# Two transformer blocks in fp32 on one core: pair sums every ten steps, earlier splits of the down weights, and another order of a norm's parts

## The reference, cut to what matters

```python
mod = jnp.dot(jax.nn.silu(c), w_ada) + b_ada
...
merged = jax.nn.sigmoid(ga) * y_a + jax.nn.sigmoid(gb) * y_r
x = x + gate1 * jnp.dot(merged, w_out)
h2 = _rmsnorm(x, norm2_w) * (1.0 + scale2) + shift2
ffn = jnp.dot(jax.nn.silu(jnp.dot(h2, w_ffn_gate)) * jnp.dot(h2, w_ffn_up), w_ffn_down)
x = x + gate2 * ffn
return _rmsnorm(x, final_norm_w)
```

## Time and profile before

| what | value |
|---|---|
| median of 3 runs | 1520.65 us (1519.39 to 1521.84) |
| profiled execution | 1521.84 us |
| its span | 1520.0 us |
| granted TensorE clock, mean | 0.994 |
| TensorE busy | 1488.0 us (98%) |
| VectorE busy | 1107.5 us (73%) |
| ACT busy | 710.9 us (47%) |

### The profile page before, as it was taken

One profiled execution on the slowest core, in us unless ns is written; L12 is line 12 of the kernel. 1 busy time (PEld: TensorE's weight loads), 2 busy tenths in 40 slices (PEclk: granted clock), 3 DMA queues, 4 the chain that ended last, 5 costly groups with the idle time before them and its releaser, 6 DMA issues.

```text
span 1520.0 us, 22717 instructions
## 1 busy us (share of the span) xinstructions
PE 1488.0 (98%) x9247; PEld 1248.8 (82%) x9247; DVE 1107.5 (73%) x1841; ACT 710.9 (47%) x1158; POOL 64.2 (4%) x93
## 2 busy tenths in 40 slices
PE   7999999999999999999999889999999999999999
PEld 5777888778877899999988777777788988888887
DVE  6669888875587698888789766787567456556885
ACT  4453334653221365455465553766525334434653
POOL 1000000000000011000000112200011000000000
PEclk9999999999999999999999989999999999999999
DMA  9423124358687678967357417850114232233473
GB/s 386 146 76 99 62 69 140 112 177 308 224 292 278 231 262 245 256 173 188 98 165 218 150 32 245 180 111 30 57 56 129 93 109 83 86 111 97 135 230 127
DMA packets 87025, 238.09 MB, mean 157 GB/s; under 512 B 12037, under 2 KB 12165, under 8 KB 85769
## 3 DMA queue, kind: packets, MB, share of 16 engines
q1 hardware_dynamic: 68312, 204.87, 39.5%
q0 software_dynamic: 18608, 31.77, 9.8%
HBM read 222.94 MB, written 45.35 MB: 177 GB/s over the span
## 4 chain that ended last, share of the span: by engine, by line
PE 85%; DVE 9%; ACT 2%; DMA 2%; issue 1%; POOL 0%; SPq 0%; DVEq 0%; ACTq 0%
PE bank L831 81%; PE bank L843 4%; DVE AR L2144 2%; DVE wl L2110 1%; DMA CST<-in_down 1%; DVE ACC L2107 1%; DVE Hl L2144 1%; ACT wh L1544 1%; DVE AR L2454 1%; DVE CST L2144 1%; DVE X L2144 0%; DVE G L2151 0%; DMA raw<-in_wst 0%; DMA X<-in_x 0%; DVE AR L2151 0%
## 5 line engine op out<-in xcount | busy, mean ns | idle before, releaser
L1544 ACT ACTIVATE wh<-raw 128x1024 fp32r<-128x1024 f32 (+1 forms) x248 | 259.0, 1046 | 335.4 <-PE bank L831 284.7
L2110 DVE TENSOR_TENSOR wl<-raw,wh 128x1024 fp32r<-128x1024 f32 (+1 forms) x248 | 297.2, 1208 | 96.9 <-ACT wh L1544 96.8
L831 PE MATMUL bank<-wh,Hh 128*128 128x512 f32 (+1 forms) x732 | 296.1, 405 | 1.5 <-DVE Hl L2144 0.7
L831 PE MATMUL bank<-wh,Hl 128*128 128x512 f32 (+1 forms) x732 | 283.9, 388 | 0.0
L831 PE MATMUL bank<-Hh,wh 128*128 128x256 f32 (+2 forms) x824 | 279.1, 339 | 4.6 <-DVE wl L2110 3.0
L831 PE MATMUL bank<-wl,Hh 128*128 128x512 f32 (+1 forms) x732 | 283.3, 387 | 0.0
L831 PE MATMUL bank<-Hl,wh 128*128 128x256 f32 (+2 forms) x824 | 277.1, 336 | 0.0
L831 PE MATMUL bank<-Hh,wl 128*128 128x256 f32 (+2 forms) x824 | 277.0, 336 | 0.0
L831 PEld LDWEIGHTS bank<-Hh,wh 128*128 128x128 f32 (+1 forms) x824 | 156.5, 190 | 22.4 <-DVE wl L2110 3.4
L831 PEld LDWEIGHTS bank<-Hl,wh 128*128 128x128 f32 (+1 forms) x824 | 156.5, 190 | 16.6 <-issue 0.5
L831 PEld LDWEIGHTS bank<-Hh,wl 128*128 128x128 f32 (+1 forms) x824 | 156.4, 190 | 16.5
(11 more groups left out here) (298 smaller groups left out, 2365.8 us busy)
## 6 DMA issues: line engine op xcount, KB each, us to landing
raw<-in_wst SPq DMA_DIRECT2D x212, 512.0 KB, 4.5
sums_dram<-in_down POOLq DMA_DIRECT2D x11, 2816.0 KB, 32.8
raw<-sums_dram SPq DMA_DIRECT2D x37, 512.0 KB, 4.1
raw<-in_down SPq DMA_DIRECT2D x25, 512.0 KB, 4.4
CST<-in_down SPq DMA_DIRECT2D x11, 1024.0 KB, 6.0
sums_dram<-CST SPq DMA_DIRECT2D x11, 1024.0 KB, 4.6
AR<-in_wst SPq DMA_DIRECT2D x8, 1024.0 KB, 10.5
CST<-in_wst SPq DMA_DIRECT2D x10, 512.0 KB, 6.5
```

Of the source, the lines that this page charges most:

```text
L831: return e.matmul(o, l, r, start=start, stop=stop, skip_group_check=True)
L1544: e.activation(HI[slot[i]][:, 0:width(i)], raw_of(i), ACT.Copy).then_inc(*w_hi.mark(i))
L2110: e.tensor_tensor(LO[slot[i]][:, 0:n], raw_of(i), HI[slot[i]][:, 0:n].bitcast(f32), SUB).then_inc(*w_lo.mark(i))
```

## The change

It has five edits.

1. The chunks of `ada` parts 4 and 5 enter the weight plan one chunk of gb1 earlier (`start=1`).
2. `summing()` places a pair's load, additions and store every ten steps instead of twelve, the additions still six steps behind the load.
3. In `schedule()` the down product takes two splits in a step from s = 4 on. The later splits and the loads of SP for them stand two steps earlier than before.
4. On VectorE, `after_dn(0)` and `after_dn(1)` are both called behind the two `upper_rows`, so that both tiles' additions stand ahead of both norms. On ACT, the square of tile 2 is placed one step after the call instead of three.
5. SP issues the loads of two bias rows (`row(4)`, `row(5)`) earlier in gb0.

```diff
@@ -84,7 +84,7 @@
     w_in("gr0 gr1 ga0 ga1", ada((2, 3), 1))
     w_in("gb0")
     among = ada((4, 5), 1)
-    block("gb1", "w_in", 8, [(6728, 512)], among=among, start=2)
+    block("gb1", "w_in", 8, [(6728, 512)], among=among, start=1)
     for n in (0, 1):
         block(f"ap{n}", "w_attn_proj", 4, [(512 * n, 512)], among=among)
     for n in (0, 1):
@@ -206,9 +206,9 @@
     load, add, store = ([[] for _ in range(len(ticks) + 2)] for _ in range(3))
     among = [k for k, t in enumerate(ticks) if t[0] in EARLY]
     for p in range(11):
-        load[among[12 * p]].append(("dn", p))
-        add[among[12 * p + 6]].append(("dn", p))
-        store[among[12 * p + 6]].append(("dn", p))
+        load[among[10 * p]].append(("dn", p))
+        add[among[10 * p + 6]].append(("dn", p))
+        store[among[10 * p + 6]].append(("dn", p))
     return load, add, store
 
 
@@ -418,7 +418,7 @@
                 ahead = 5 if name != "iq" else 3 if what[0] == 7 else what[0] % 2
                 if not avail or rank[at] > here + ahead + 3 * (name == "up"):
                     break
-                if name == "dn" and hi_at[k]:
+                if name == "dn" and len(hi_at[k]) > (what[0] > 3):
                     break
                 soon = at in (i, ticks[k + 1][2])
                 if mine and loaded.get(at, -9) + 2 > k and not soon:
@@ -1893,7 +1893,7 @@
                     on.wait_ge(*dve.of(("dn", "left", 20)))
                     e.activation(xn, X[:, t, :], ACT.Square, scale=1.0 / 32, accum_out=ss).then_inc(*act.mark(("last", "mean", t)))
                 if t == 2:
-                    w.after(3, root)
+                    w.after(1, root)
                 else:
                     root()
                 w.after((3, 4, 4, 4)[t], lambda: norm_root("n3", t, dve.of(("last", "x", t))))
@@ -2758,7 +2758,9 @@
                         added(SGR[2 + r], SGR[2 + r], "5", r, "v")
                     if s == 35:
                         w.after(3, lambda r=r: upper_rows(r))
-                        after_dn(r)
+                        if r:
+                            after_dn(0)
+                            after_dn(1)
                     if s == (42, 47)[r]:
                         added(SGR[r], SGR[r], "4", r, "c21 4")
                         gated(SGR[r], 0, 2 + r, ("dn", "x", 2 + r))
@@ -3262,9 +3264,9 @@
                         compression(2)
                         on.wait_ge(*small.of(("comp", 0)))
                         compression(3)
-                    if name == "gb0" and what == (2, 0):
+                    if name == "gb0" and what == (1, 3):
                         row(4)
-                    if name == "gb0" and what == (2, 2):
+                    if name == "gb0" and what == (2, 1):
                         row(5)
                     if name == "2dn" and what[0] in FINISHED:
                         event, rows, h, n = FINISHED[what[0]]
```

## The result

| | before | changed |
|---|---|---|
| median | 1519.97 us (1518.82 to 1521.84, 6 runs) | 1526.45 us (1523.54 to 1531.46, 6 runs) |
| ratio of the times | | 1.0043, 95% interval 1.0024 to 1.0062 |
| profiled execution, its span | 1521.84, 1520.0 us | 1523.63, 1521.8 us |

The changed kernel is 6.5 us slower by the medians, where 2.6 us of gain were forecast. Its times are spread over 8 us, those of before over 3. The profiled execution of the changed kernel is one of its two fastest and that of the kernel before is its slowest, so the two profiles show only a part of the loss, 1.8 us, but they show where it lies.

A forecast was written before the change was run, and what follows sets the result against it. TensorE, busy 98% of the span, was taken as the bound, so only its waits and low clock could be regained. Region 2's -2.1 and region 1's -0.5 gave -2.6 us from the median 1520.65: 1518.1 us, range 1513.6 to 1522.8.

The forecast's parts named there:

- Region 2: Down product's end and its norms: norm_scale(2) and TensorE's turn 2 come sooner, -2.1 us (bounds -1.0 and -3.5).
- the wait before turn 0: Third norm: TensorE waits some 4.1 us for norm_scale(0), where it lost 5.2 before; slow matmuls stay.
- POOL and the lock: Rival at the norms: POOL done only with the additions, norms 1.2 us later, 1519.3 us in all; chance 0.10.
- Region 1: Stretch with pairs every ten steps: four terms for sums ahead of what TensorE needs, -0.5 us (bounds -6.4 and +6).
- (a): Sum at 443.76, ahead of a bank read: it stands earlier; of TensorE's 1.6 us wait 0.8 is gained.
- (d): Pair 10's sum at step 290, just before wo0's wl: new wait, 0.7 us lost.
- Part 3: Pairs every ten steps: SP stands about 1.5 us at nearly every pair load, raw weight loads queued behind.
- (b): wl at 475.10, ending the 3.0 us wait: one sum comes ahead, another goes; -1.1 us (ends -4.8 and +0.6).
- (c): Pair 4's sum ahead of a wl of gb1, near 400: new wait, 0.7 us lost.
- The signs of being wrong: TensorE waits less than 2 us before turn 0, or the sums' load waits grow with each pair.
- The rival that came true: Slower by the buffer's round: above 14.8 us, each pair later, sums meet wl of gb1, rp1, wo0; +5.7, written 1525; chance 0.12.
- The page's price for 1 MB: Pair loads: 4.4 us each by the page, a round of 11.5 us, region 1 would give 4 us; not used.

The follow-up runs named there:

- e1: Kernel before with only the three edits of the down product (two splits a step, additions ahead of norms, third square sooner): 1517.72 us, ratio 0.9988.
- e5: Kernel before with only two splits a step in the down product; norms stay between the additions, third square late: 1521.70 us, ratio 1.0012.
- e3: Kernel before with only the pairs placed every ten steps instead of twelve: 1528.50 us, ratio 1.0055.
- e16: Kernel before with pair 1's load one step sooner, exchanged with ga1.2's raw load on SP's queue, nothing else: 1525.30 us, ratio 1.0032.
- e15: Kernel before with pairs every ten steps, loads after the first two steps later (10p + 2), sums and stores at 10p + 8: 1528.54 us, ratio 1.0048.
- e10: Kernel before with pairs every ten steps, but pair 1 left at its old place (12 and 18): 1526.72 us, ratio 1.0041.
- e13: Kernel before with pair 1's load at step 10 instead of 12, its sum at 16, and half that load's bytes: 1524.75 us, ratio 1.0021.
- e4: Kernel before with only the ada chunks one place sooner and the bias rows sooner, pairs every twelve steps: 1520.89 us, ratio 0.9995.
- e7: Kernel before with only the third tile's square two steps sooner: 1519.88 us, ratio 0.9994.
- e17: e10 with pair 6's load four steps later, behind five raw loads, its sum three later, pairs 7 and 8 shifted: 1533.51 us, ratio 1.0080.
- e11: Kernel before with every pair's sum and store eight steps behind the load instead of six, spacing twelve: 1518.31 us, ratio 0.9980.
- e2: Kernel before with only the three stream edits (pairs every ten steps, ada chunks and bias rows sooner): 1529.84 us, ratio 1.0060.

## Why the prediction was wrong

**Region 2, -2.1 us:** right in mechanism, somewhat small. Additions, `last_norm`, both norm scales and the wait before turn 0 came within 1 us of their forecast places. Turn 2 came 2.4 us sooner for 2.1. The rest of the 3.2 measured is the clock: the wait before turn 2 was 2.6 us instead of 3.9, and the slow matmuls behind it cost 0.8 less, where I had kept them all. I had the wait as longer than before because TensorE would be 3 us ahead; it was 1.0 ahead. The low clock now covers the transposes of turns 0 and 1: their rows take 1.97 and 1.84 us, before 1.04 and 1.03. e1 gives 3.0 in the median and 1.8 by the ratio. e5 confirms that splitting sooner does not by itself gain the 5.2 us.

**POOL and the lock:** no sign of starvation. The rival that POOL ends only with the last addition is refuted: `last_norm(0)` started straight behind the last addition, with no idle time for POOL. In the changed kernel POOL's second operation takes 0.99 us beside the additions and 0.57 alone, so it is held for some 0.4 us and not to the end of the row.

**Region 1, -0.5 us:** this step failed; it measured +5.8 in the trace and +7.8 in e3's median. The sum of terms (a) to (d) looked only at what stands behind a sum on VectorE. It left out the queue on which the moved load is issued. Part 3 said that SP would stand "with the loads of raw weights queued behind it", and put no price on it. The largest loss, 4.5 us in the trace and 4.9 by e16, comes of it: pair 1's load passes ga1.2's. The next, 1.9 us at 431, is on the same queue: a raw load behind a pair load for which SP stood. The trace of before had the evidence: ACT already waited 1.69 us for ga1.2's data at 347.40, so this load had no slack, and the order of SP shows what overtakes it. Of the terms: (a) the gap at 445 fell from 1.6 to 1.0 us, and the stretch around it gained 0.3, where I took 0.8; (b) the wait at rp1.3 is 2.7 for 3.0 us, worth 0.4, and its slow matmuls stay, where I took 1.1, and executions of one program differ there by more; (c) near 400 and (d) at wo0 there is no stall in the changed kernel's trace, both were 0 of the 0.7 each; (d)'s stall did appear in e15.

The signs of being wrong did not show it either: TensorE waited 3.4 us before turn 0, and the sums' waits did not grow from pair to pair (4.3, 0, 3.2, 0, 1.7, 7.9, 0, 0.7, 3.0, 0 and 1.4 us). SP stood for the store at 7 pair loads and not at 11. No sign watched the raw loads.

**The rival that came true** had its chance at 0.12, its price about right (+5.7; 6.5 measured) and its mechanism half right: VectorE stood at sums (22.1 us for 13.8) and raw loads queued behind. It had each pair later than the one before, by rounds above the spacing, and the sums head on against `wl` of gb1, rp1 and wo0; the trace has one such round in eleven and no new stall at these three. It missed the overtaken load, so that its price came out is in part luck. The range ended at 1522.8, half way to this rival's 1525, though region 1's own bound of +6 with region 2's -2.1 gives 1524.6; the measured 1526.45 is beyond that too.

**The page's price for 1 MB** (4.4 us by the Trainium skill's fit, "DMA: Bandwidth & Descriptors", "Anatomy of one DMA — SWDGE (gpsimd) path", for the other kind of queue) was rightly not used: the pair loads of e10 took 4.9 to 8.5 us, with a median of 5.9. No run here uses that other kind of queue for such a load.

## What to carry to other kernels

When a transfer is moved on a queue, list the transfers that it overtakes and look in the trace at which of their readers already waits for data: a reader with a wait of 1.7 us has no slack for a megabyte in front. Price what the reader's engine has queued behind it as well; here a bank copy that needed nothing from the transfer held TensorE. Where one buffer is loaded, used and stored in turn, look at the loads that stand behind each of its steps on the queue, and not only at whether the round fits: here it did for ten of eleven pairs. When two traces are compared, see first how much the place in question differs between executions of the same program. A wait removed in front of a chain of norms is worth what the chain then gives: work the chain out to its end before counting the wait.

## What the runs showed of the hardware that was not expected

- With three loads issued together, 1 MB and two of 512 KB, the third took 6.6 us to its use instead of 4.0, while the 16 DMA engines were busy all the time (a share of 1.02 in the stretch) and moved 420 GB/s (the changed kernel, 344 to 349); with 512 KB less in front it still took 6.2 (e13, 344.33 to 350.52).
- The length of a wait does not by itself decide whether the clock falls. In the traces of all the kernels here from 60 us on, the clock stayed at 1.00 behind every wait of TensorE of up to 1.9 us and fell behind every one of 2.95 us or more. In between it did either: it fell behind 1.95 us (e4, rp1.3) and stayed at 1.00 behind 1.96 (e7, rp1.3); it stayed behind 2.56 (e13), 2.69 (e17), 2.71 (e11) and 2.74 us (e2, rp1.3) and fell behind 2.70 (e1) and 2.74 us (the changed kernel, twice). At 348 in the changed kernel the fall cost some 1.7 us beyond the 2.7 waited. What decides in between no run here shows.
